# A backbone of two layers: scatters with a bound on the row, and the second layer's rows kept in the output tensor

## The chip, the cores and the metric

The kernel runs on one core of a Trainium2 chip. The metric is the device time of one execution in microseconds (us); lower is better. The core has a matrix engine (TensorE, PE in the rows), a vector engine (VectorE, DVE), an activation engine (ScalarE, ACT), GpSimd (POOL), SyncE (SP), which only issues transfers and waits, and 16 DMA engines that all queues share. Transfers issued by SyncE and ScalarE go over hardware queues (q1, q10), those of GpSimd over the software queue (q0).

## What is computed

Two layers over 1024 latent tokens of width 1024, in float32: a Fourier mixer, then a short gated convolution, each followed by a mixture of 16 experts of which every token uses two. Context tokens don't reach the output in this depth. Cut to what matters here:

```python
x = x + g1 * mixer(norm(x) * (1 + sc1) + sh1)          # layer 0: Fourier, layer 1: convolution
h = norm(x) * (1 + sc2) + sh2
comb = weights of the two chosen experts of each token   # (1024, 16), two entries per row
y = 0
for e in range(16):
    y = y + comb[:, e:e+1] * ((silu(h @ w_gate[e]) * (h @ w_up[e])) @ w_down[e])
x = x + g2 * y                                           # after layer 1 this is the output
```

## The kernel before, in words

**Stages.** Layer 0's Fourier mixer, its router, its experts; then layer 1's convolution, router and experts. After each mixer the residual rows x are stored in a tensor in device memory, x_dram[layer], and the normalized rows h in h_dram[layer]. Both are kept there because the experts read and add rows in an order that the router decides.

**The experts.** The 2048 pairs of a token and an expert are sorted by expert and cut into slots of 128 rows, an expert's pairs beginning a new slot. With 16 experts there are at most MAX_SLOTS = 31 slots; how many are used is read from a register, and the loops skip the others by twos. A slot's pairs fill its rows from row 0 on; the rows left over are padding. TOKI holds for each slot (a column) the token of each row (a partition), and for a padding row SEQ + partition, 1024 to 1151, by a minimum with the constant column C_SPARE.

Of each slot, GpSimd gathers its 128 rows of h into XG (line 577, four slots ahead), with a bound of SEQ - 1 on the row, so padding is skipped. TensorE transposes XG (line 1782), multiplies by gate and up weights (line 1792), transposes the hidden rows (line 1798) and multiplies by down weights (lines 1805, 1811). VectorE evicts the result, weighted, into one of two tiles YO (line 1370). GpSimd scatters YO with addition into x_dram[layer] (line 588); each scatter waits for the landing of the one before. Padding rows are added to 128 spare rows that x_dram has behind its 1024.

**SyncE's queue** holds the loads of expert weights in the order of the experts: gate and up into RAW (line 451), down into WDR (line 455), two buffers each, a load waiting until the buffer's expert is done. After layer 0's experts it reads x_dram[0] back into X (line 505). After layer 1's experts, line 528 copies the first 1024 rows of x_dram[1] to the output, as 64 pieces of 64 KB, and waits for that.

**Signals.** x_stored[layer] counts the stores of x (8 tiles) and the fill of the spare rows (`fill_spare_rows`, lines 416 to 419, issued by GpSimd near the start as ones from the constants K). y_scattered[layer] counts landings of scatters, moe_done is raised once all of a layer's have landed.

```python
if s:
    pool.wait_ge(y_scattered[layer], 16 * s)
    pool.sem_inc(y_added, 1)
pool.indirect_dma_start(out=x_dram[layer], out_offset=bass.IndirectOffsetOnAxis(ap=TOKI[:, s:s + 1], axis=0),
                        in_=YO[s % 2][:], in_offset=None, compute_op=ALU.add
                        ).then_inc(y_scattered[layer], 16)
```

Of the kernel before, what the change touches and what calls it, by code (L numbers as in the profile page):

```python
# [23 lines left out]
P = 128  # L24
SEQ, D = 1024, 1024
NT = SEQ // P
NC = D // P
# [98 lines left out]
def backbone(nc, x, c, w_ada, b_ada, norm_mix, norm_ffn, fourier_w_out, conv_w_in, conv_w, conv_w_out,  # L126
             router_w, router_bias, moe_w_gate, moe_w_up, moe_w_down, tables, constants, out):
    f32, f32r, i32, u32 = mybir.dt.float32, mybir.dt.float32r, mybir.dt.int32, mybir.dt.uint32
    ALU, ACT, X_AXIS = mybir.AluOpType, mybir.ActivationFunctionType, mybir.AxisListType.X
# [3 lines left out]
    def sem(name):  # L133
        return top.enter_context(nc.semaphore(name))
# [18 lines left out]
    x_rows, out_rows = x[0], out[0]  # L153
# [11 lines left out]
    ident, ones, lower = (K[:, a:a + P] for a in (C_IDENT, C_ONES, C_LOWER))  # L165
# [28 lines left out]
    r = Region(rows_at)  # L194
    FAB = r.put("FAB", [P, 2, D])
    FAA = r.put("FAA", [P, 2, D])
    r = Region(fourier_at)
# [12 lines left out]
    r = Region(fa_at)  # L210
# [3 lines left out]
    r = Region(fold_at)  # L214
# [3 lines left out]
    r = Region(fourier_at)  # L218
# [5 lines left out]
    r = Region(phase)  # L224
# [7 lines left out]
    r = Region(base)  # L232
    WDR = r.put("WDR", [P, 2, FF // P, D])
    XG = [r.put(f"XG{i}", [P, D]) for i in range(2)]
    YO = [r.put(f"YO{i}", [P, D]) for i in range(2)]
# [4 lines left out]
    r = Region(ada_at - width(SQ.shape))  # L240
# [6 lines left out]
    r = Region(ada_at)  # L247
# [49 lines left out]
    def bank(i, n=1):  # L297
# [1 line left out]


    h_dram = [nc.dram_tensor(f"h_dram{i}", [SEQ, D], f32, kind="Internal").ap() for i in range(2)]
    x_dram = [nc.dram_tensor(f"x_dram{i}", [SEQ + P, D], f32, kind="Internal").ap() for i in range(2)]


    consts_in, small_in, c_in, tables_in = sem("consts_in"), sem("small_in"), sem("c_in"), sem("tables_in")
    vectors_in, vectors_tr, warm = sem("vectors_in"), sem("vectors_tr"), sem("warm")
    bias_in, norm_row_in, out_done = (
        sem(n) for n in ("bias_in", "norm_row_in", "out_done"))
    wf_in = [sem(f"wf_in{i}") for i in range(2)]
    wm_in = [sem(f"wm_in{i}") for i in range(2)]  # L310
    wn_in = sem("wn_in")
# [101 lines left out]

        return 2 if layer == 0 and m % 2 else 4

    def fill_spare_rows(pool, layer):

        rows = x_dram[layer].rearrange("s (c n) -> s c n", n=P)
        pool.dma_start(rows[SEQ:SEQ + P, :, :], ones[:, None, :].to_broadcast([P, NC, P])).then_inc(x_stored[layer], 16)

    def slots_used(engine):

        return engine.value_load(SEID[0:1, MAX_SLOTS:MAX_SLOTS + 1], min_val=PAIRS // P, max_val=MAX_SLOTS)
# [2 lines left out]
    def _(sp):  # L426
# [30 lines left out]
        for layer in range(2):  # L457
            for m in range(0, NT, 1 if layer else 2):
                sp.wait_ge(h_ready, layer * NT + m + 1)
                sp.dma_start(rows_of(h_dram[layer], layer, m), h_tile(layer, m)[:]).then_inc(h_stored[m % 4], 16)  # L460
            sp.wait_ge(y_mm, NT * (layer + 1))
            load_gate_up(layer, 0, 0)
            load_gate_up(layer, 1, 1)
            sp.wait_ge(x_stored[layer], 16 * (NT + 1))
            load_down(layer, 0, 0)
            sp.wait_ge(routed, layer + 1)
            b = layer * MAX_SLOTS

            def after_split(e):
                sp.wait_ge(w_low, end_of(e) * PIECES + b * PIECES)  # L470

            def after_down(e):
                sp.wait_ge(yd_mm, end_of(e) + b)

            after_split(0)
            load_gate_up(layer, 2, 0)
            load_down(layer, 1, 1)
            after_split(1)
            load_gate_up(layer, 3, 1)
            after_down(0)  # L480
            load_down(layer, 2, 0)
            with sp.Fori(2, HALF) as j:
                for k in range(2):
                    after_split(2 * j + (k - 2))
                    load_gate_up(layer, 2 * j + k, k)
                    after_down(2 * j + (k - 3))
                    load_down(layer, 2 * j + (k - 1), 1 - k)
            after_down(EXPERTS - 3)
            load_down(layer, EXPERTS - 1, 1)
            if layer == 0:  # L490
                def load_win(j, part, par):

                    src = conv_w_in[0].rearrange("(c p) (s n) -> p c s n", p=P, s=3)[:, :, part, ds(j * P, P)]
                    sp.dma_start(WINR[par][:], src).then_inc(win_in[par], 16)

                def load_ada_pair(piece, half):

                    for k in range(2):
                        sp.wait_ge(wa_used, 4 * piece + (N_ADA + 2 * half + k - 1))
                        load_ada(sp, 1, piece, 2 * half + k, k)  # L500

                load_ada_pair(2, 0)
                sp.wait_ge(moe_done, 1)
                for m in range(NT):
                    sp.dma_start(X[:, m, :], x_dram[0][m * P:(m + 1) * P, :]).then_inc(x_back[m], 16)
                load_win(0, PARTS[0], 0)
                load_win(0, PARTS[1], 1)
                sp.wait_ge(cin_mm, 1)
                load_win(0, PARTS[2], 0)
                for n in range(3):  # L510
                    sp.wait_ge(cin_mm, n + 2)
                    load_win(1, PARTS[n], (n + 1) % 2)
                with sp.Fori(1, NC // 2) as i:
                    for k in range(2):
                        for n in range(3):
                            sp.wait_ge(cin_mm, 6 * i + (3 * k + n - 1))
                            sp.sem_inc(win_free, 1)
                            load_win(2 * i + k, PARTS[n], (k + n) % 2)
                            if n == 0:
                                load_ada_pair(i + (1 + k), 1 - k)  # L520
                load_ada_pair(5, 1)
                sp.wait_ge(cin_mm, 3 * NC)
                for q in range(4):
                    sp.dma_start(WOR[:, 2 * q:2 * q + 2, :],
                                 conv_w_out[0, 2 * q * P:2 * (q + 1) * P, :].rearrange("(j p) n -> p j n", p=P)
                                 ).then_inc(wout_in[q], 16)
        sp.wait_ge(moe_done, 2)
        sp.dma_start(out_rows.rearrange("(p r) d -> p (r d)", p=P),
                     x_dram[1][0:SEQ, :].rearrange("(p r) d -> p (r d)", p=P)).then_inc(out_done, 16)
        sp.wait_ge(out_done, 16)  # L530

    @block.gpsimd
    def _(pool):
# [5 lines left out]
        bias_row(0)  # L539

        pool.wait_ge(consts_in, 16)
        for layer in range(2):
            fill_spare_rows(pool, layer)

        pool.wait_ge(folds, 5)
        for g in range(GROUPS):
            pool.indirect_dma_start(out=WM[:, g, :], out_offset=None, in_=fourier_w_out[0],
# [34 lines left out]
        def scatter(layer, s):  # L582

            pool.wait_ge(yo_ready, s + (layer * MAX_SLOTS + 1))
            if s:
                pool.wait_ge(y_scattered[layer], 16 * s)
                pool.sem_inc(y_added, 1)
            pool.indirect_dma_start(out=x_dram[layer], out_offset=bass.IndirectOffsetOnAxis(ap=TOKI[:, s:s + 1], axis=0),  # L588
                                    in_=YO[s % 2][:], in_offset=None, compute_op=ALU.add
                                    ).then_inc(y_scattered[layer], 16)  # L590

        def slot(layer, s):
# [5 lines left out]
        for layer in range(2):  # L598
# [16 lines left out]
            gather(layer, 1, 1)  # L615
            pool.wait_ge(routed, layer + 1)
            used = slots_used(pool)
            pool.wait_ge(x_stored[layer], 16 * (NT + 1))
            if layer == 0:
                bias_row(1)  # L620
            for s in range(2):
# [1326 lines left out]
```

## Time and profile before

| what | value |
|---|---|
| median of 3 runs | 1252.8 us (1250.09 to 1255.69) |
| profiled execution | 1256.65 us, its span 1254.7 us |
| TensorE busy | 1119.3 us, 89% of the span |
| VectorE busy | 848.2 us, 68% |
| ScalarE busy | 490.6 us, 39% |
| GpSimd busy | 209.6 us, 17% |
| SyncE's and ScalarE's queues, GpSimd's queue | 38.2% and 2.9%, 18.0% of 16 DMA engines |
| chain that ended last | TensorE 69%, VectorE 9%, DMA 9%, issue 4%, ScalarE 4% |

The profile is one execution. The span runs from the first to the last record of the core. An engine's busy share doesn't tell what ends a stage; the chain of waits does, which is followed back from the last instruction to whatever released it. A transfer's time to landing runs from its issue to the moment when all 16 DMA engines have reported.

### The profile page before, as it was taken

What the parts mean: (1) busy time and instruction counts of PE and PEld (TensorE: products, weight loads), DVE (VectorE), ACT (ScalarE), POOL (GpSimd) and SP (SyncE); (2) the same over time, 40 slices, a digit from 0 to 9 for tenths busy, and PEclk for the clock granted to TensorE, in tenths of its full rate; (3) what the DMA queues carried; (4) which work ended last, traced back from release to release, by engine and by line L of the source; (5) the groups of instructions that cost most, each with busy time, mean ns of one, the idle gap of its engine ahead of it and who ended that gap; (6) DMA issues with size and microseconds to landing.
All of it is one profiled execution on the core that took longest, in us unless ns stands there. A gap on an engine that the chain in (4) does not pass through costs nothing.

```text
span 1254.7 us, 16332 instructions
## 1 busy us (share of the span) xinstructions
PE 1119.3 (89%) x4749; PEld 821.8 (65%) x4750; DVE 848.2 (68%) x976; ACT 490.6 (39%) x676; POOL 209.6 (17%) x140
## 2 busy tenths in 40 slices
PE   3999998899799899769999999979997799889991
PEld 1544456666567677458888888848885677667761
DVE  4886987789798799364444444463656788599782
ACT  5210233555556566341111111142222466476661
POOL 2201120322323333100000000000000132223331
PEclk9989999799989999879999999989998699999996
DMA  9859235489979987701333323231225569998946
GB/s 372 339 203 384 114 130 222 164 271 291 372 213 293 339 256 213 202 1 51 118 118 117 115 104 116 101 150 51 98 88 201 224 199 301 345 318 259 305 91 168
DMA packets 82170, 251.39 MB, mean 200 GB/s; under 512 B 8640, under 2 KB 33416, under 8 KB 73740
## 3 DMA queue, kind: packets, MB, share of 16 engines
q1 hardware_dynamic: 59604, 180.48, 38.2%
q0 software_dynamic: 18784, 56.69, 18.0%
q10 hardware_dynamic: 3736, 13.65, 2.9%
q8 instruction: 23, 0.38, 0.1%
q14 instruction: 23, 0.19, 0.0%
HBM read 220.39 MB, written 46.14 MB: 212 GB/s over the span
## 4 chain that ended last, share of the span: by engine, by line
PE 69%; DVE 9%; DMA 9%; issue 4%; ACT 4%; DVEq 1%; ACTq 1%; SPq 1%; POOL 0%; POOLq 0%
PE PS L1792 15%; PE PS L1700 7%; PE PS L1896 7%; PE PS L1900 7%; PE PS L1897 7%; DMA RAW<-in_moe_w_up_dram 6%; PE PS L1805 4%; PE PS L1811 3%; PE PS L1782 3%; PE PS L1568 2%; PE PS L1651 2%; PE PS L1668 2%; PE PS L1713 2%; DVE WL L1356 2%; ACT WH L842 1%
## 5 line engine op out<-in xcount | busy, mean ns | idle before, releaser
L1356 DVE TENSOR_TENSOR WL<-RAW,WH 128x1024 fp32r<-128x1024 f32 x204 | 240.0, 1219 | 37.7 <-ACT WH L842 31.1
L842 ACT ACTIVATE WH<-RAW 128x1024 fp32r x196 | 196.4, 1054 | 55.0 <-DMA RAW<-in_moe_w_up_dram 47.7
L1792 PE MATMUL PS<-WH,XTH 128*128 128x512 f32 x384 | 160.0, 417 | 20.7 <-DVE XTL L1349 11.8
L1896 PE MATMUL PS<-HTH,WINH 128*128 128x512 f32 x384 | 150.7, 393 | 5.4 <-DVE HTL L1476 5.4
L1792 PE MATMUL PS<-WL,XTH 128*128 128x512 f32 x384 | 155.4, 405 | 0.0
L1792 PE MATMUL PS<-WH,XTL 128*128 128x512 f32 x384 | 155.4, 405 | 0.0
L1897 PE MATMUL PS<-HTL,WINH 128*128 128x512 f32 x384 | 149.9, 390 | 0.0
L588 POOL DMA_INDIRECT x_dram<-YO,TOKI x46 | 99.1, 2154 | 300.1 <-DVE YO L1370 128.3
L1900 PE MATMUL PS<-HTH,WINL 128*128 128x512 f32 x384 | 118.7, 390 | 0.0
L1792 PEld LDWEIGHTS PS<-WH,XTH 128*128 128x128 f32 x384 | 75.7, 197 | 40.8 <-issue 25.9
L1041 DVE SCALAR_TENSOR_TENSOR ACC<-WA,SC,ACC 128x1024 f32 (+1 forms) x72 | 92.4, 1283 | 7.4 <-DMA WA<-in_w_ada_dram 3.2
L1805 PE MATMUL PS<-WDR,HETF 128*128 x184 | 88.4, 604 | 7.5 <-DVE YO L1370 7.5
L567 POOL DMA_DIRECT2D x_dram<-X x12 | 6.6, 553 | 502.2 <-DVE X L1112 433.9
L577 POOL DMA_INDIRECT XG<-h_dram,TOKI x54 | 68.5, 1269 | 125.9 <-PE PS L1782 64.8
L1792 PEld LDWEIGHTS PS<-WH,XTL 128*128 128x128 f32 x384 | 75.5, 197 | 16.9
L1896 PEld LDWEIGHTS PS<-HTH,WINH 128*128 128x128 f32 x384 | 72.3, 188 | 21.7 <-DVE HTL L1476 4.8
L1792 PEld LDWEIGHTS PS<-WL,XTH 128*128 128x128 f32 x384 | 75.6, 197 | 14.8
L1900 PEld LDWEIGHTS PS<-HTH,WINL 128*128 128x128 f32 x384 | 72.4, 188 | 15.1
L1897 PEld LDWEIGHTS PS<-HTL,WINH 128*128 128x128 f32 x384 | 72.4, 189 | 14.8
L1349 DVE TENSOR_TENSOR XTL<-PS,XTH 128x1024 fp32r<-128x1024 f32 x50 | 61.0, 1221 | 22.6 <-ACT XTH L833 22.5
L833 ACT ACTIVATE XTH<-PS 128x1024 fp32r<-128x1024 f32 x50 | 51.2, 1025 | 54.8 <-PE PS L1782 54.2
L929 ACT ACTIVATE WINH<-WINR 128x1024 fp32r<-128x1024 f32 x24 | 25.4, 1060 | 112.9 <-DMA WINR<-in_conv_w_in_dram 112.9
(230 smaller groups left out, 1737.0 us busy)
## 6 DMA issues: line engine op xcount, KB each, us to landing
RAW<-in_moe_w_gate_dram SPq DMA_DIRECT2D x32, 1024.0 KB
RAW<-in_moe_w_up_dram SPq DMA_DIRECT2D x32, 1024.0 KB
WDR<-in_moe_w_down_dram SPq DMA_DIRECT2D x32, 1024.0 KB
WA<-in_w_ada_dram SPq DMA_DIRECT2D x28, 1024.0 KB
WAE<-in_w_ada_dram SPq DMA_DIRECT2D x12, 1024.0 KB, 12.0
WINR<-in_conv_w_in_dram SPq DMA_DIRECT2D x24, 512.0 KB, 3.8
WA<-in_w_ada_dram ACTq DMA_DIRECT2D x8, 1024.0 KB
x_dram<-X POOLq DMA_DIRECT2D x12, 512.0 KB, 2.9
```

Source lines behind the costliest of these rows:

```text
L577: pool.indirect_dma_start(out=XG[par][:], out_offset=None, in_=h_dram[layer], in_offset=bass.IndirectOffsetOnAxis(ap=TOKI[:, s:s + 1], axi ...
L588: pool.indirect_dma_start(out=x_dram[layer], out_offset=bass.IndirectOffsetOnAxis(ap=TOKI[:, s:s + 1], axis=0), in_=YO[s % 2][:], in_offse ...
L842: nc.scalar.activation(piece_of(WH[par], i), raw_piece(e, i), ACT.Copy).then_inc(w_high, 1)
L1041: ins = V.scalar_tensor_tensor(out=dst, in0=WA_ALL[par][:, k, :], scalar=SC[:, at:at + 1], in1=dst, op0=ALU.mult, op1=ALU.add)
L1349: V.tensor_tensor(XTL[:].rearrange("p c n -> p (c n)"), bank(0, 2), XTH[:].rearrange("p c n -> p (c n)").bitcast(f32), ALU.subtract).then_ ...
L1356: V.tensor_tensor(piece_of(WL[par], i), raw_piece(e, i), piece_of(WH[par], i).bitcast(f32), ALU.subtract).then_inc(w_low, 1)
L1700: ins = T.matmul(bank(b + h), z[m % 2][:, ch, :], w[:, ch, h * BANK:(h + 1) * BANK], start=ch == 0 and i == 0, stop=ch == NC - 1 and i == 2)
L1792: ins = T.matmul(bank(2), x[:, ch, :], w[par][:, :, ch, :], start=ch == 0 and i == 0, stop=ch == NC - 1 and i == 2)
L1805: T.matmul(bank(4 + h), HETF[:], W[:, h * BANK:(h + 1) * BANK], start=True, stop=False)
L1896: T.matmul(bank(b), WINH[par][:, ch, :], HTH[:, ch, cols], start=ch == 0, stop=False)
L1897: T.matmul(bank(b), WINH[par][:, ch, :], HTL[:, ch, cols], start=False, stop=False)
L1900: ins = T.matmul(bank(b), WINL[par][:, ch, :], HTH[:, ch, cols], start=False, stop=ch == NC - 1)
```

## The change

Four edits that belong together. x_dram[0] has 1024 rows instead of 1152, and x_dram[1] is the output tensor itself. Each scatter has a bound of SEQ - 1 on the row and skips rows above it. The fills of the spare rows and their count in x_stored go. The copy from x_dram[1] to the output and the wait for it go; SyncE still waits for moe_done. TOKI and everything on TensorE, VectorE and ScalarE stay as they are.

```diff
-    x_dram = [nc.dram_tensor(f"x_dram{i}", [SEQ + P, D], f32, kind="Internal").ap() for i in range(2)]
+    x_dram = [nc.dram_tensor("x_dram", [SEQ, D], f32, kind="Internal").ap(), out_rows]
...
-    def fill_spare_rows(pool, layer):
-
-        rows = x_dram[layer].rearrange("s (c n) -> s c n", n=P)
-        pool.dma_start(rows[SEQ:SEQ + P, :, :], ones[:, None, :].to_broadcast([P, NC, P])).then_inc(x_stored[layer], 16)
...
-            sp.wait_ge(x_stored[layer], 16 * (NT + 1))
+            sp.wait_ge(x_stored[layer], 16 * NT)
...
         sp.wait_ge(moe_done, 2)
-        sp.dma_start(out_rows.rearrange("(p r) d -> p (r d)", p=P),
-                     x_dram[1][0:SEQ, :].rearrange("(p r) d -> p (r d)", p=P)).then_inc(out_done, 16)
-        sp.wait_ge(out_done, 16)
...
-        for layer in range(2):
-            fill_spare_rows(pool, layer)
-
...
-                                    in_=YO[s % 2][:], in_offset=None, compute_op=ALU.add
+                                    in_=YO[s % 2][:], in_offset=None, bounds_check=SEQ - 1, oob_is_err=False,
+                                    compute_op=ALU.add
...
-            pool.wait_ge(x_stored[layer], 16 * (NT + 1))
+            pool.wait_ge(x_stored[layer], 16 * NT)
```

On SyncE, the end of the program, behind the loop over the experts of layer 1. Before, the load of the last down weights is followed by the copy and the wait for it:

```order
190 L473 REGISTER_ALU
191 L455 DMA WDR<-in_moe_w_down_dram 128x2x1024 [waits yd_mm]
192 L528 DMA out_dram<-x_dram 64x16384 [waits moe_done]
193 L1924 UNCONDITIONAL_BRANCH [waits out_done]
```

After, the block ends on moe_done:

```order
190 L467 REGISTER_ALU
191 L449 DMA WDR<-in_moe_w_down_dram 128x2x1024 [waits yd_mm]
192 L1913 UNCONDITIONAL_BRANCH [waits moe_done]
```

One transfer and one wait have left the queue, and nothing stands in their place.

On GpSimd, the last scatters of layer 1 and the end of its program, before and then after:

```order
198 L588 DMA x_dram<-YO_109,TOKI 1152x1024 [waits yo_ready,y_scattered1]
199 L588 DMA x_dram<-YO_110,TOKI 1152x1024 [waits yo_ready,y_scattered1]
200 L588 DMA x_dram<-YO_109,TOKI 1152x1024 [waits yo_ready,y_scattered1]
201 L636 UNCONDITIONAL_BRANCH [waits y_scattered1]
```

```order
196 L576 DMA out_dram<-YO_109,TOKI 1024x1024 [waits yo_ready,y_scattered1]
197 L576 DMA out_dram<-YO_110,TOKI 1024x1024 [waits yo_ready,y_scattered1]
198 L576 DMA out_dram<-YO_109,TOKI 1024x1024 [waits yo_ready,y_scattered1]
199 L625 UNCONDITIONAL_BRANCH [waits y_scattered1]
```

The order and the waits are the same; the target is out, and 1024 rows are in reach instead of 1152.

## Rows read from the trace of the kernel before

**Rows 1.** The page: its head, TensorE's busy time, the chain that ended last.

```profile
span 1254.7 us, 16332 instructions
...
PE 1119.3 (89%) x4749; PEld 821.8 (65%) x4750; DVE 848.2 (68%) x976; ACT 490.6 (39%) x676; POOL 209.6 (17%) x140
...
PE 69%; DVE 9%; DMA 9%; issue 4%; ACT 4%; DVEq 1%; ACTq 1%; SPq 1%; POOL 0%; POOLq 0%
```

**Rows 2.** The chain's last stretch in order of time: start us, us, what.

```profile
1209.25 5.48 PE PS L1792 x24
...
1218.93 5.49 PE PS L1792 x24
...
1230.55 1.29 DVE YO L1370
...
1232.66 1.58 POOL x_dram L588
```

**Rows 3.** SyncE's instructions at the end: start us, us, engine, line, operation.

```profile
1239.07 0.63 SPq L528 DMA_DIRECT2D out_dram<-x_dram  x1
```

**Rows 4.** What SyncE waited for: us in total, times, longest us.

```profile
SPq L528 <- POOLq L644: 43.2, 1, 43.2
...
SPq L1924 <- DMA out_dram<-x_dram: 14.6, 1, 14.6
```

**Rows 5.** DMA traffic from 1232 to 1255: queues, then issues with us to landing.

```profile
q1 hardware_dynamic: 80, 4.19, 54.7%
q0 software_dynamic: 144, 0.52, 15.1%
...
x_dram<-YO,TOKI POOLq DMA_INDIRECT x1, 6.2
out_dram<-x_dram SPq DMA_DIRECT2D x1, 15.2
```

**Rows 6.** Line 567, the stores of x: duration ns min/median/max, then landing.

```profile
L567 POOL DMA_DIRECT2D x_dram<-X x12: 531/540/615, 127.6 to 947.4; - x12
...
DMA to landing us min/median/max: 2.9/2.9/5.1
```

**Rows 7.** Line 588, the scatters: both layers, landing, then layer 1 alone.

```profile
L588 POOL DMA_INDIRECT x_dram<-YO,TOKI x46: 1575/1866/4218, 253.5 to 1232.7; - x46
...
DMA to landing us min/median/max: 6.0/9.1/14.1
...
L588 POOL DMA_INDIRECT x_dram<-YO,TOKI x22: 1575/1828/4203, 1011.0 to 1232.7; - x22
```

**Rows 8.** DMA traffic from 1206 to 1212, with the packets' sizes.

```profile
DMA packets 288, 0.52 MB, mean 87 GB/s; under 512 B 160, under 2 KB 160, under 8 KB 288
```

**Rows 9.** The chain's transfers in the expert loops and between the layers.

```profile
257.19 10.52 DMA RAW<-in_moe_w_up_dram
...
320.70 14.48 DMA RAW<-in_moe_w_up_dram
...
413.92 11.99 DMA RAW<-in_moe_w_up_dram
...
508.07 6.58 DMA x_dram<-YO,TOKI
...
516.55 7.09 DMA X<-x_dram
...
1058.46 12.40 DMA RAW<-in_moe_w_up_dram
...
1082.93 13.05 DMA RAW<-in_moe_w_up_dram
...
1161.72 12.57 DMA RAW<-in_moe_w_up_dram
```

**Rows 10.** Busy times of two stretches; the last three columns: clock, DMA share, GB/s.

```profile
1058.00:1072.00 14.00, 14.00 (x63) 10.53 (x61) 7.69 (x9) 5.23 (x7) 3.60 (x3) 1.00 0.96 329
...
1161.00:1175.00 14.00, 14.00 (x63) 10.31 (x62) 10.48 (x12) 8.21 (x11) 3.49 (x2) 1.00 0.97 311
```

**Rows 11.** DMA traffic of the same stretches, 1058 to 1072, then 1161 to 1175.

```profile
q0 software_dynamic: 288, 0.85, 25.0%
...
x_dram<-YO,TOKI POOLq DMA_INDIRECT x2, 11.4
...
q0 software_dynamic: 420, 1.47, 37.9%
...
x_dram<-YO,TOKI POOLq DMA_INDIRECT x1, 11.5
```

**Rows 12.** Indirect transfers without a bound (564, 572) and with (577): ns min/median/max.

```profile
L564 POOL DMA_INDIRECT x_dram<-X,K x4: 973/1390/1885, 128.8 to 185.7; - x4
...
L572 POOL DMA_INDIRECT h_dram<-H,K x4: 950/954/1542, 164.9 to 195.4; - x4
...
L577 POOL DMA_INDIRECT XG<-h_dram,TOKI x54: 984/1040/2079, 219.1 to 1226.1; - x54
```

**Rows 13.** GpSimd's last two instructions, with the idle time before each.

```profile
1226.07 1.02 POOL L577 DMA_INDIRECT XG<-h_dram,TOKI  x1 [1.28 <-PE PS L1782]
1232.66 1.58 POOL L588 DMA_INDIRECT x_dram<-YO,TOKI  x1 [5.57 <-DVEq L1415]
```

**Rows 14.** GpSimd near the start: the fills of spare rows, the next work.

```profile
19.32 1.83 POOL L419 DMA_DIRECT2D x_dram<-K  x2 [12.36 <-DMA K<-in_constants_dram]
32.12 2.24 POOL L547 DMA_INDIRECT WM<-in_fourier_w_out_dram,K  x1 [10.98 <-DVE FAB L1027]
```

**Rows 15.** VectorE's first use of the WA blocks.

```profile
35.71 5.31 DVE L1041 SCALAR_TENSOR_TENSOR ACC<-WA,SC,ACC 128x1024 f32<-128x1024 f32 x4
```

More of the change, by code:

```diff
@@ L301, in backbone @@
     h_dram = [nc.dram_tensor(f"h_dram{i}", [SEQ, D], f32, kind="Internal").ap() for i in range(2)]
-    x_dram = [nc.dram_tensor(f"x_dram{i}", [SEQ + P, D], f32, kind="Internal").ap() for i in range(2)]
+    x_dram = [nc.dram_tensor("x_dram", [SEQ, D], f32, kind="Internal").ap(), out_rows]
     consts_in, small_in, c_in, tables_in = sem("consts_in"), sem("small_in"), sem("c_in"), sem("tables_in")
     vectors_in, vectors_tr, warm = sem("vectors_in"), sem("vectors_tr"), sem("warm")
-    bias_in, norm_row_in, out_done = (
-        sem(n) for n in ("bias_in", "norm_row_in", "out_done"))
+    bias_in, norm_row_in = sem("bias_in"), sem("norm_row_in")
     wf_in = [sem(f"wf_in{i}") for i in range(2)]
```

## The prediction

> **What bounds the kernel now.** I read the page's head first: one core, a span of 1254.7 us, TensorE busy for 89% of it, and TensorE with 69% of the chain of work that ended last; DMA holds 9% of that chain [rows 1]. The profiled execution took 1256.65 us, so 1.95 us lie around the span. That execution is 3.85 us above the median of 1252.8 us, so I work out a difference on its trace and take it off the median.
>
> The second view is the chain at its end. The last matrix products of the last slot lead to the eviction of YO (1230.55, 1.29 us) and to GpSimd's last scatter, issued at 1232.66 [rows 2]. The third view is SyncE's queue: the next thing in the program is one transfer, out from x_dram, issued at 1239.07 [rows 3], and the only thing after it is SyncE's 14.6 us wait for that transfer [rows 4]. The landing times say the same: the last scatter lands 6.2 us after its issue (1232.66 + 6.2 = 1238.9), the copy 15.2 us after its own (1239.1 + 15.2 = 1254.3), and the span ends 0.4 us later [rows 3, 5]. From 1238.9 no compute engine works; the end of the kernel is a serial transfer.
>
> **The copy of the output goes.** In after, layer 1 stores its rows in out and adds the experts' rows there, so the transfer of line 528 has no successor: SyncE waits for moe_done and the block ends. Of the old tail, 1239.1 to 1254.3 disappears, and the 0.4 us from the last landing to the end of the span stay. That is 15.2 us, all of it on the path, with no cover to look for and nothing late next except the last scatter, which was there before. Eight stores of 512 KB (x_dram from X, 540 ns each on GpSimd, 2.9 us to landing) change their destination and nothing else [rows 6]. Term: **-15.2 us**.
>
> A rule of the Trainium skill can be set beside this row. DMA: Bandwidth & Descriptors, "Anatomy of one DMA", fits a transfer from GpSimd's queue as 2.0 us plus its bytes at 436 GB/s; for the 4.19 MB that the copy moves this would be 11.6 us, where the trace has 15.2 [rows 5]. By the page the kernel would gain 3.6 us less; the row decides, since it is the very transfer that is removed.
>
> **The rows that pad a tile.** The loop issues 46 scatters of 128 rows (22 of them in layer 1), 5888 rows, of which 2 x 2048 are pairs of a token and an expert [rows 7]. The other 1792 rows, 30%, are padding: before, they are added to 128 spare rows; now their index is above the bound and they are skipped. What a skipped row costs is seen in the gathers, which have the same bound already. The stretch 1206 to 1212 holds one whole scatter and a gather for a slot that isn't used: 160 packets under 512 B and 128 others, 0.52 MB in all [rows 8]. So 128 skipped rows became 128 tiny packets and moved nothing.
>
> What a full scatter costs the DMA engines is seen in 1232 to 1255, where it is all that the software queue carries: 144 packets take 15.1% of 16 engines over 23 us, 3.5 us of each engine [rows 5]. The padding of a mean scatter is 30% of that, 1.06 us. It pays only where a transfer ends last. The chain names the places: six waits for gate and up weights (RAW), of 10.52, 14.48, 11.99, 12.40, 13.05 and 12.57 us, 75.0 us together [rows 9]. In two of these stretches the DMA share is 0.96 and 0.97 [rows 10], so the engines really are full there, and software-queue traffic takes 25.0% and 37.9% of them [rows 11]. Of scatters, the first stretch issues 2 and the second 1, say 1.5 for each wait. If relief went straight to the waits it would be 6 x 1.5 x 1.06 = 9.6 us. The other bound is 0: a load of weights is complete only when its slowest engine is, and the padding isn't spread evenly, since a slot's pairs fill its tile from row 0 and padding is always the last rows. Below nothing it can't go by this term, as packets only become smaller. I take a fifth of the upper end, because all engines must be relieved for a wait to end earlier. Term: **-2 us**, bounds -9.6 and 0.
>
> The Trainium skill has a rule against this gain: DMA: Bandwidth & Descriptors, "The descriptor swizzle", gives each DMA engine eight fixed partitions, engines 0 to 7 those below 64 and 8 to 15 those above. By it engine 0 keeps its eight rows in every tile with 36 or more pairs, and the term would be near 0 (1237.6 us in all). The page of the profile doesn't tell engines apart, so no row here shows it.
>
> Outside these waits less padding buys nothing. The only scatter that the chain holds whole inside the program is the last of layer 0 (508.07, 6.58 us, followed by 7.09 us for the way back into X) [rows 9]. Counted with the reference's own router on its inputs, the last expert's last tile has 121 pairs in layer 0 and 58 in layer 1: 7 and 70 padding rows. The first gives nothing. The second could shorten the very last landing by up to 70/128 of 3.5 us, 1.9 us, or not at all if one engine has only real rows; that is inside the bounds above.
>
> **The bound on the row.** Each scatter now has its indices compared with 1023. GpSimd spends 1575 to 4218 ns on a scatter [rows 7]. The price of the comparison lies between rows with and without it: indirect transfers without a bound take at least 950 and 973 ns, gathers with one at least 984 [rows 12], and 1.02 us where every row is skipped (the last gather, at 1226.07) [rows 13]. That is 0.01 to 0.05 us a piece; a loss of 0.05 x 46 = 2.3 us would need all to be exposed. Only the last one of each layer is, since otherwise GpSimd stood idle before its scatter, for 5.57 us before the last one [rows 13]. So 0.1 us at most, taken as 0.
>
> **The two fills of spare rows** at 19.3 us go (two instructions, 1.83 us of GpSimd, 2 x 512 KB). Nobody waits: GpSimd's next work, WM, starts at 32.12 after an idle time of 10.98 us for VectorE's FAB, and VectorE takes the first WA blocks at 35.71 with no idle time before it [rows 14, 15]. The saved transfers make the loads that were already queued land earlier, ahead of any reader. The final wait for x_stored has one landing less to count, and that landing was some 30 us in. Term: 0.
>
> **Sum.** -15.2 - 2 + 0 + 0 = -17.2 us. The profiled execution would have taken 1256.65 - 17.2 = 1239.5 us (span 1237.5); the median comes to 1252.8 - 17.2 = **1235.6 us**, 1.4% faster.
>
> **Rivals.** *Relief where it counts* (chance 0.22). The slowest DMA engine in the RAW waits is one that serves last rows, and gets rid of most of its padding. For: a share of 0.96 leaves little but those waits to shorten, and in 1161 to 1175 the software queue has 38% of the engines. Against: nothing shows which engine is last. With 5 to 10 us instead of 2 the time is 1227.6 to 1232.6; I put it at 1230. The skill's DMA: Bandwidth & Descriptors ("DMA engines 7/15 usually slower") would favour this, as it names the engine with the highest partitions as a slow one.
>
> *The bound is dear, or out is a slightly slower target* (0.08): 1 to 3 us of the copy's gain are lost at the exposed scatters and in slots where the next scatter waits on a landing: 1238 to 1240. For it speaks that no trace here has bound and addition together.
>
> *Scatters into out become the bound* (0.04, slower). Each scatter waits for the landing of the one before, so a slot can't be shorter than issue plus landing. TensorE's slot is 9.7 us (1209.25 to 1218.93) [rows 2]; the last scatter landed in 6.2, the median in 9.1 [rows 5, 7]. If the output tensor took additions so slowly that a landing passes 9.7 us even in quiet slots, each of the 22 slots of layer 1 pays the excess: at 10.4 the copy's gain is used up (22 x 0.7 = 15.2), beyond 10.7 the kernel is slower by over 0.5%, and at 11.5, the figure beside full loads [rows 11], it is 1252.8 - 15.2 + 40 = 1277.6. Against: both tensors are device memory, and the copy wrote out at full share.
>
> *The tail comes back in another form* (0.04, no change): the end of the kernel waits for something that the copy hid, such as a late completion of writes to out. The price can be up to the copy's own 15.2 us: about 1250.
>
> **How the numbers follow.** The forecast as summed has 0.62, from 1233.6 to 1237.6. Relief 0.22, dear bound 0.08, no change 0.04, slower 0.04. The median itself stands on runs from 1250.09 to 1255.69, some 3 us either way. The range 1228 to 1240 holds the first three but for their edges. A measurement of this kernel can tell about 0.5%, 6.3 us, from no change. Faster by more than that: 0.62 + 0.22 + 0.08 = 0.92; same 0.04; slower 0.04.
>
> **What would show it.** In the profile after: no transfer from x_dram to out, and the span ending within half a microsecond of the last scatter's landing; the last scatter at 6.2 us or a little less to landing, and 1575 ns still the least that a scatter takes on GpSimd. The software queue should carry about 1792 x 4 KB = 7.3 MB less, plus 1 MB of fills. The six RAW waits tell the second term: 73 us in sum for my forecast, 65 for the rival. If scatters of layer 1 take longer to land than those of layer 0 in quiet slots, out is the slower target. My number is wrong if the end of the chain isn't the last scatter, or if the RAW waits lose more than 5 us.

## The result, and the profile after

| kernel | median | lowest to highest | runs |
|---|---|---|---|
| before | 1253.09 us | 1249.5 to 1260.78 | 7 |
| after | 1242.95 us | 1240.95 to 1245.62 | 7 |

The ratio of after to before is 0.9918, with a 95% interval of 0.9892 to 0.9944: 10.3 us faster, between 7.0 and 13.5. The forecast was 17.2 us less, and its range ended at 1240. The sign was right, the size was not. The profiled execution of after took 1242.95 us, the median itself, with a span of 1241.0 us.

The head of the page, the DMA queues, and the chain that ended last, after; they answer to [rows 1]:

```profile
span 1241.0 us, 16376 instructions
...
PE 1114.6 (90%) x4749; PEld 820.0 (66%) x4750; DVE 848.0 (68%) x976; ACT 491.1 (40%) x676; POOL 207.5 (17%) x138
...
q1 hardware_dynamic: 59524, 176.29, 37.5%
q0 software_dynamic: 18496, 48.32, 15.2%
...
PE 72%; DVE 9%; DMA 8%; issue 4%; ACT 3%; DVEq 1%; ACTq 1%; SPq 1%; POOL 0%; POOLq 0%
```

The software queue q0 carries 48.32 MB. In the page of before it carried:

```profile
q0 software_dynamic: 18784, 56.69, 18.0%
```

These are 8.37 MB less, as forecast (1792 rows of 4 KB and 1 MB of fills). So padding rows and fills are gone. The copy is gone from q1, which carried 180.48 MB before. The tail is where the surprise lies. The last piece of the chain of after, which answers to [rows 2]:

```profile
1226.90 1.57 POOL out_dram L576
```

What SyncE waited for in after (us in total, times, longest), answering to [rows 4]:

```profile
SPq L1913 <- POOLq L633: 42.6, 1, 42.6
...
SPq L1913 <- PEq L1913: 7.1, 1, 7.1
```

There is no wait for a copy, but there is a new one of 7.1 us in the line on which the program's block ends. The instructions of that line in after (duration ns min/median/max, first and last start in us) name its cause:

```profile
L1913 ACTq DRAIN  x1: 8/8/8, 1226.5 to 1226.5; - x1
L1913 PEldq DRAIN  x1: 8/8/8, 1226.7 to 1226.7; - x1
L1913 DVEq DRAIN  x1: 17/17/17, 1230.3 to 1230.3; - x1
L1913 SPq COMPARE_BRANCH  x1: 38/38/38, 1233.7 to 1233.7; - x1
L1913 POOLq DRAIN  x1: 7017/7017/7017, 1233.7 to 1233.7; - x1
L1913 SPq DRAIN  x1: 7/7/7, 1233.9 to 1233.9; - x1
L1913 SPq EVENT_SEMAPHORE  x1: 17/17/17, 1240.9 to 1240.9; - x1
```

Every engine ends its program with an instruction called DRAIN and then meets the others. Those of the other engines take 7 to 17 ns; GpSimd's starts when the last scatter has landed (1233.7) and takes 7017 ns. The others wait for it until 1240.9, where the span ends. The row names PEq as the releaser, since the wait is put down to the last to arrive at the meeting; the rows of the line show that it was GpSimd that came late. The same line in before:

```profile
L1924 POOLq DRAIN  x1: 7017/7017/7017, 1239.1 to 1239.1; - x1
L1924 SPq COMPARE_BRANCH  x1: 38/38/38, 1254.3 to 1254.3; - x1
L1924 SPq DRAIN  x1: 7/7/7, 1254.5 to 1254.5; - x1
```

It was there all the time, from 1239.1 to 1246.1, beside the copy, which ran until 1254.3. Taking the copy away uncovered it.

### The profile page after: what moved, and what is told of

It reads as the page before. It is cut to its first block, busy times and chain, and to the rows that moved or that the text cites. A ratio compares the mean times of both kernels' runs of the same rounds, so it can differ in the third digit from the quotient of the medians.

```text
span 1241.0 us, 16376 instructions
## 1 busy us (share of the span) xinstructions
PE 1114.6 (90%) x4749; PEld 820.0 (66%) x4750; DVE 848.0 (68%) x976; ACT 491.1 (40%) x676; POOL 207.5 (17%) x138
## 3 DMA queue, kind: packets, MB, share of 16 engines
q0 software_dynamic: 18496, 48.32, 15.2%
## 4 chain that ended last, share of the span: by engine, by line
PE 72%; DVE 9%; DMA 8%; issue 4%; ACT 3%; DVEq 1%; ACTq 1%; SPq 1%; POOL 0%; POOLq 0%
PE PS L1781 16%; PE PS L1689 7%; PE PS L1885 7%; PE PS L1889 7%; PE PS L1886 7%; PE PS L1794 4%; PE PS L1800 3%; DMA RAW<-in_moe_w_up_dram 3%; PE PS L1771 3%; PE PS L1557 2%; PE PS L1640 2%; PE PS L1657 2%; PE PS L1702 2%; DVE WL L1345 2%; DVE ACC L1030 1%
## 5 line engine op out<-in xcount | busy, mean ns | idle before, releaser
L565 POOL DMA_INDIRECT XG<-h_dram,TOKI x54 | 71.2, 1319 | 129.2 <-PE PS L1771 67.6
L1781 PEld LDWEIGHTS PS<-WL,XTH 128*128 128x128 f32 x384 | 75.2, 196 | 14.7
L576 POOL DMA_INDIRECT x_dram<-YO,TOKI x24 | 51.9, 2165 | 151.5 <-DVE YO L1359 123.2
L555 POOL DMA_DIRECT2D out_dram<-X x8 | 4.3, 543 | 432.7 <-DVE X L1101 432.7
```

Source lines behind the costliest of these rows:

```text
L565: pool.indirect_dma_start(out=XG[par][:], out_offset=None, in_=h_dram[layer], in_offset=bass.IndirectOffsetOnAxis(ap=TOKI[:, s:s + 1], axi ...
L1781: ins = T.matmul(bank(2), x[:, ch, :], w[par][:, :, ch, :], start=ch == 0 and i == 0, stop=ch == NC - 1 and i == 2)
```

## Experiments

Ratios are against the kernel before, which was timed in turn with each group of kernels on the same chip. Its own median lay between 1252.8 and 1255.9 us from group to group, so times of two groups are compared by their ratios. "Us less" is a ratio's distance from 1, times the median of the kernel before.

**after_again** is the changed kernel once more, the reference for no_copy, keep_copy and drain_early, which were timed with it on one chip.

> The changed kernel once more, beside the three others on one chip. Both theories: about 1243 us, 10 us under the kernel before (1253.1). It is the reference for the others: GpSimd's last instruction of the program (DRAIN, 7017 ns in both traces) starts when the last scatter has landed and ends at the end of the span.

Measured: 1244.25 us beside 1254.67 us; ratio 0.9907, 0.9873 to 0.9941. As expected.

**no_copy** is the kernel before without its copy; it leaves the output unwritten.

```diff
         sp.wait_ge(moe_done, 2)
-        sp.dma_start(out_rows.rearrange("(p r) d -> p (r d)", p=P),
-                     x_dram[1][0:SEQ, :].rearrange("(p r) d -> p (r d)", p=P)).then_inc(out_done, 16)
-        sp.wait_ge(out_done, 16)
```

> The kernel before, spare rows, fills and unbounded scatters included, without the copy at its end; it leaves the output unwritten. Theory D: the tail goes from 15.2 us to the 7.1 us of the DRAIN, 8.1 us under before, 1245.0 us. My prediction's step (only 0.4 us lie behind the last landing): 15.2 us under before, 1237.9 us.

Measured: 1246.61 us, ratio 0.9924 (0.9896 to 0.9951), so 9.5 us less than before (6.1 to 13.0). The 8.1 us of theory D lie in that interval, the 15.2 us of my step don't. The line on which its block ends shows the DRAIN in the open, with the end of the span behind it:

```profile
L1921 POOLq DRAIN  x1: 7017/7017/7017, 1240.5 to 1240.5; - x1
...
L1921 SPq EVENT_SEMAPHORE  x1: 17/17/17, 1247.7 to 1247.7; - x1
```

**keep_copy** is the other part alone: the bound, no spare rows, no fills, but a tensor of its own for layer 1 and the copy.

```diff
-    x_dram = [nc.dram_tensor("x_dram", [SEQ, D], f32, kind="Internal").ap(), out_rows]
+    x_dram = [nc.dram_tensor(f"x_dram{i}", [SEQ, D], f32, kind="Internal").ap() for i in range(2)]
...
         sp.wait_ge(moe_done, 2)
+        sp.dma_start(out_rows.rearrange("(p r) d -> p (r d)", p=P),
+                     x_dram[1][0:SEQ, :].rearrange("(p r) d -> p (r d)", p=P)).then_inc(out_done, 16)
+        sp.wait_ge(out_done, 16)
```

> One part of the change alone: bound on the row, no spare rows, no fills; layer 1 still collects its rows in a tensor of its own, and the copy to the output stays. Theory D with a small relief of the DMA engines: 2 us under before, 1251 us. Rival (large relief, as the last scatter starts 5.8 us earlier in the trace of after than in that of before): 5 to 6 us under before, about 1247.5 us. If the bound cost anything that shows: at or over 1253 us.

Measured: 1251.56 us, ratio 0.9977 (0.9953 to 1.0001): 2.9 us less than before, between 5.9 less and none. The small relief is favoured, the large one is just inside the edge. The run measures bound and relief together, so by itself it only excludes a bound that costs more than the relief brings. No_copy and keep_copy together give 9.5 + 2.9 = 12.4 us; after gained 11.7 on this chip. The two parts add up.

**pool_waits** makes GpSimd wait for the copy in the kernel before, so that its DRAIN can't hide.

```diff
             pool.sem_inc(y_added, 1)
             pool.sem_inc(moe_done, 1)
+        pool.wait_ge(out_done, 16)
```

> The kernel before, with one wait more: GpSimd waits for the copy to the output before its program ends, so that its closing DRAIN can't run beside the copy. Theory D (fixed 7.0 us, hidden under the copy in before): 7.0 us over before, about 1261.5 us, with a DRAIN of 7017 ns behind the copy. Rival (the DRAIN's length is what is left of GpSimd's own transfers, long landed by then): a DRAIN well under 1 us and the time of before, 1254.7 us.

Measured: 1259.97 us beside 1255.28, ratio 1.0048 (1.0025 to 1.0071): 6.0 us more, between 3.1 and 8.9. The DRAIN of 7014 ns stands behind the copy:

```profile
L1925 SPq DRAIN  x1: 7/7/7, 1251.3 to 1251.3; - x1
L1925 POOLq DRAIN  x1: 7014/7014/7014, 1251.3 to 1251.3; - x1
```

The last scatter was issued at 1229.6 and landed 6.4 us later, so this DRAIN starts 15 us after the last landing of GpSimd's own transfers. It is as long there as right behind a landing. It isn't the remainder of a transfer under way.

**drain_early** is after, with GpSimd's last wait given to SyncE.

```diff
             with pool.Else():
-                pool.wait_ge(y_scattered[layer], (used + (used & 1)) * 16)
+                if layer == 0:
+                    pool.wait_ge(y_scattered[layer], (used + (used & 1)) * 16)
                 pool.sem_inc(y_added, MAX_SLOTS - 2 * PAIR_LOOPS)
             pool.sem_inc(y_added, 1)
-            pool.sem_inc(moe_done, 1)
+            if layer == 0:
+                pool.sem_inc(moe_done, 1)
...
-        sp.wait_ge(moe_done, 2)
+        used = slots_used(sp)
+        with sp.If(used > 2 * PAIR_LOOPS):
+            sp.wait_ge(y_scattered[1], 16 * MAX_SLOTS)
+        with sp.Else():
+            sp.wait_ge(y_scattered[1], (used + (used & 1)) * 16)
+            sp.sem_inc(moe_done, 1)
```

> As after, but in layer 1 GpSimd no longer waits for the landing of the last scatter; SyncE does. Theory D (the 7.0 us of GpSimd's closing DRAIN is a fixed time that the copy hid and that is now in the open): the DRAIN starts right behind the issue of the last scatter, some 5.2 us earlier (in the trace of after 1228.5 instead of 1233.7), and the kernel takes 5.2 us less than after, about 1237.8 us. Rival (the DRAIN first waits until GpSimd's transfers have landed and then takes its 7.0 us): the DRAIN becomes about 12 us long and the time stays at 1243 us.

Measured: 1240.33 us, ratio 0.9877 (0.9845 to 0.991). The median is 3.9 us below that of after_again, but with 5 and 4 executions whose ranges overlap (1238.2 to 1245.0 and 1242.4 to 1245.3) the times alone don't prove a gain. Neither theory came true as written: the DRAIN starts before the landing and takes 9721 ns.

```profile
L1921 POOLq DRAIN  x1: 9721/9721/9721, 1231.2 to 1231.2; - x1
...
L1921 SPq DRAIN  x1: 7/7/7, 1236.5 to 1236.5; - x1
```

SyncE, which waits for the landing, is at its own DRAIN at 1236.5; GpSimd's ends at 1240.9. What SyncE waits for at the end is now

```profile
SPq L1921 <- PEq L1921: 4.7, 1, 4.7
```

4.7 us instead of 7.1. So 2.4 us of what the DRAIN does had been done before the landing. Spread_early below, built the same way, shows 4.7 us again, with a DRAIN of 7973 ns. In the traces the time from the issue of the last scatter to the end of the span falls from 1241.0 - 1226.9 = 14.1 us to 1241.2 - 1230.2 = 11.0 us; 0.4 us of that are a landing 0.4 us sooner (6.2 against 6.6 us).

**Six small programs** ask what the DRAIN is made of. In them SyncE copies x to the output as one transfer, and GpSimd issues a number of 512 KB loads into one tile, each waiting for the one before. They compute nothing of the backbone, and each was run once.

```python
for i in range(LOADS):
    pool.dma_start(T0[:], x_rows[(i % 8) * P:(i % 8 + 1) * P, :]).then_inc(loaded, 16)
    pool.wait_ge(loaded, 16 * (i + 1))
pool.wait_ge(copied, 16)
```

> Not the backbone: one core, SyncE copies x to the output in one transfer, GpSimd clears a tile, issues no transfer and waits for the copy. It asks how long GpSimd's closing DRAIN is. If it is 7.0 us in any program: 7.0. If it is the price of having issued transfers: under 0.5 us, like the DRAIN at the start of the traces (183 ns).

> Not the backbone: SyncE copies x to the output, GpSimd clears a tile, issues one load of 512 KB, waits for its landing and for the copy, and ends. Without any transfer of GpSimd the closing DRAIN took 41 ns. Theory D (a fixed price of having issued transfers): 7.0 us behind the copy, the kernel 7 us longer than the 18.04 us without. Rival (the DRAIN grows with the number of transfers or descriptors, 118 transfers in the backbone): well under 1 us.

> As micro_pool1, but 40 loads one after another. Theory D: again 7.0 us, no matter how many. Rival: longer than for one load.

> As micro_pool40, with 80 loads. The DRAIN took 41, 135 and 3327 ns behind 0, 1 and 40 transfers, 82 ns for each one more. Theory N (it grows with the number of GpSimd's transfers): 3327 + 40 x 82 = 6.6 us. Rival (it stops growing earlier, or depends on the kind of transfer, and the 7.0 us of the backbone have another source): 3.3 us again or anything else.

> As micro_pool80, with 130 loads, the number of transfers that GpSimd issues in the changed backbone (132 in the kernel before). Theory N with a cap (the backbone shows 7017 ns with 132 as with 130): 7.0 us. Without a cap 3327 + 90 x 82 = 10.7 us; the backbone's 7.0 us would then be another thing.

(The backbone issues 130 transfers on GpSimd after the change and 132 before; the 118 in one expectation was a wrong count.) The closing DRAINs with 0, 1, 40, 80 and 130 loads:

```profile
L33 POOLq DRAIN  x1: 41/41/41, 16.0 to 16.0; - x1
```

```profile
L33 POOLq DRAIN  x1: 135/135/135, 17.1 to 17.1; - x1
```

```profile
L33 POOLq DRAIN  x1: 3327/3327/3327, 166.3 to 166.3; - x1
```

```profile
L33 POOLq DRAIN  x1: 6599/6599/6599, 324.4 to 324.4; - x1
```

```profile
L33 POOLq DRAIN  x1: 1454/1454/1454, 520.6 to 520.6; - x1
```

Both fixed-price theories fall: the DRAIN grows by (6599 - 3327) / 40 = 82 ns for each transfer that GpSimd has issued, although every one has landed by then. And it doesn't grow for ever: with 130 it is 1454 ns, the worth of 17. Something had been put away on the way, some 113 transfers. The trace of this program shows where. What GpSimd was idle for before its loads (us in total, times), and the load behind the odd one (start us, us, idle time before it):

```profile
  DMA T<-in_x_dram: 440.3, 128
  issue: 6.1, 1
```

```profile
454.73 0.54 POOL L29 DMA_DIRECT2D T<-in_x_dram  x1 [6.05 <-issue]
```

Once, and only once, GpSimd stands still for 6.05 us where it mostly waits 3.2 to 3.6 us for a landing, and for nothing that the profile names. The load behind this pause is the 114th, so 113 had been issued: the number that the DRAIN gave. The program with 80 loads has no such pause.

**micro_pool1_unwaited** issues one load and lets GpSimd end at once.

> As micro_pool1, but GpSimd waits for nothing after it has issued the load, so its DRAIN starts at once, beside the copy of some 15 us. In drain_early the DRAIN was 9.7 us and ended 4.6 us after the last landing would be expected, in spread_early 8.0. If the DRAIN is 7.0 us behind the end of the engine's own work (writing the descriptors, 1 to 2 us): about 8 to 9 us, hidden under the copy, and the kernel takes 18 us. If it is 7.0 us behind the landing: about 10 us or more, still hidden.

Its DRAIN lasts as long as its transfer is under way (landing 14.7 us after the issue at 2.0):

```profile
L32 POOLq DRAIN  x1: 14832/14832/14832, 2.0 to 2.0; - x1
```

So GpSimd's DRAIN waits for its engine's transfers even where the program doesn't. (SyncE's copy ran at the same time, but it isn't what the DRAIN waits for: in before the DRAIN ended at 1246.1, beside a copy under way until 1254.3.) The kernel took 18.97 us beside 19.26 with the waits.

**extra20 and extra40** add tiny loads on GpSimd's queue to after, ahead of layer 1's stores, where the engine is idle for some 340 us.

```diff
+    SPENT = keep.put("SPENT", [P, 8])
     SQ = keep.put("SQ", [P, D])
...
             if layer:
+                for i in range(20):
+                    pool.dma_start(SPENT[:], tables[:, 0:8]).then_inc(spent, 16)
+                    pool.wait_ge(spent, 16 * (i + 1))
                 for m in range(NT):
                     store_x(layer, m)
```

> As after, with 20 tiny loads more on GpSimd's queue (4 KB each, into a tile that nobody reads) in the middle of the kernel, where GpSimd has nothing to do for 300 us. The DRAIN of 7017 ns would be (7017 - 41) / 82 = 85 transfers that are still to be put away. Theory N (a list that is put away at the end, and now and then on the way, when it is full: 130 transfers left only 1454 ns, the worth of 17, so it was emptied behind some 113): 20 more make 7017 + 20 x 82 = 8.66 us and the time 1.6 us longer. Rival (7.0 us is a ceiling in this kernel, or these transfers don't count): 7017 ns again.

> As extra20, with 40 tiny loads. Theory N: 85 + 40 = 125 passes 113, the list is emptied on the way and 12 are left: a DRAIN of about 1.0 us, and the kernel takes 6 us less than after, 1238 us. Rival: 7017 ns or 10.3 us, and 1244 to 1247 us.

Measured: one run of extra20 at 1252.1 us; extra40 1253.18 us, ratio 1.0007 (0.999 to 1.0024), where after stood at 0.9907 and 0.9918. So extra40 is 11 to 12 us slower than after, not 6 us faster. The DRAINs:

```profile
L1917 POOLq DRAIN  x1: 6527/6527/6527, 1243.3 to 1243.3; - x1
```

```profile
L1917 POOLq DRAIN  x1: 6404/6404/6404, 1243.3 to 1243.3; - x1
```

6527 ns with 20 and 6404 with 40. More transfers made it shorter, by 490 and 613 ns, but not in the way of the simple count. The length does respond to transfers issued more than 600 us earlier. Theory N's count fails in both (8.66 and about 1.0 us were expected), and so does the rival's 7017 ns; when the list is emptied in the backbone stays open.

The slowdown of both has nothing to do with the end. Their products of 128x512 take longer throughout, which the groups of the convolution show; first after, then extra40:

```profile
L1886 PE MATMUL PS<-HTL,WINH 128*128 128x512 f32 x384 | 149.9, 390 | 0.0
L1889 PE MATMUL PS<-HTH,WINL 128*128 128x512 f32 x384 | 118.8, 390 | 0.0
```

```profile
L1890 PE MATMUL PS<-HTL,WINH 128*128 128x512 f32 x384 | 151.1, 394 | 0.0
L1893 PE MATMUL PS<-HTH,WINL 128*128 128x512 f32 x384 | 120.6, 395 | 0.0
```

390 ns became 394 and 395, and TensorE is busy for 1126.8 and 1126.3 us in extra20 and extra40 against 1114.6 in after, which is the size of the loss. It is neither the loads nor the clock: the last of the loads was issued at 570.1 and 622.9 us, but between 650 and 830 us, at a granted clock of 1.00 in all three, these products still take 389 ns in after and 393 to 397 in the other two. What differs there is that SPENT takes 32 bytes of each partition and moves all tiles laid out behind it. That this is the cause is argued from two kernels that share it, and wasn't tried by itself.

**spread** asks on which DMA engines the padding falls. It is after with another order of a slot's rows on the partitions, so that padding is dealt out by fours to partitions that, by the Trainium skill's DMA: Bandwidth & Descriptors ("The descriptor swizzle"), belong to different DMA engines.

```diff
-    t[:, C_ROW:C_ROW + P] = -i
+    rank = np.zeros(P, np.int64)
+    n = 0
+    for k in range(8):
+        for e in range(16):
+            at = 64 * (e // 8) + 4 * (e % 8) + 32 * (k // 4) + k % 4
+            rank[at] = n
+            n += 1
+    t[:, C_ROW:C_ROW + P] = -rank
```

> As after, but a slot's rows are laid on the partitions in another order (the constant row numbers are permuted), so that by the Trainium skill's swizzle (DMA: Bandwidth & Descriptors, The descriptor swizzle) the padding of a tile is shared by all 16 DMA engines instead of falling on the engines of the last rows. Theory S (in the waits for RAW the slowest DMA engine is one that serves first rows, so the padding that after skips hardly helps): every engine now gets rid of its share of scatter and gather, about 1.5 us a slot, over the waits for RAW 5 to 9 us; 1236 to 1239 us. Rival (it doesn't matter which engine the padding falls on, or the order of rows has nothing to do with engines): the same as after, 1244 us.

Measured: 1237.78 us beside 1255.28, ratio 0.986 (0.9831 to 0.9889). After stood at 0.9907, so the order of rows alone is worth some 6 us (between 0.3 and 11.5, with both intervals taken into account); drain_early and spread_early, which differ in the same way, are 7.4 us apart by their ratios. The last scatter shows the effect by itself: it has the same 58 rows of tokens in both kernels. DMA traffic at the end of after, then at the end of spread (us to landing last):

```profile
out_dram<-YO,TOKI POOLq DMA_INDIRECT x1, 6.6
```

```profile
DMA packets 145, 0.25 MB, mean 19 GB/s; under 512 B 86, under 2 KB 86, under 8 KB 144
...
out_dram<-YO,TOKI POOLq DMA_INDIRECT x1, 5.0
```

In before, with all 128 rows moved, it took 6.2 us [rows 5]. Skipping 70 of 128 rows brought nothing while they were the last rows; dealt out over the partitions, the same skip brought 1.6 us. The other traces agree: 6.0 to 6.6 us in the six with the 70 rows skipped at the end, 5.0 and 4.4 us in the two with them dealt out (spread and spread_early). The swizzle of the Trainium skill fits these rows: by it the first 58 partitions give six of the 16 engines their full eight rows, and the dealt order gives none more than four.

The change also shows in the loads of weights. What ScalarE, which takes the first of the weights, waited for them (us in total, times, longest) in before, after and spread:

```profile
ACT WH L842 <- DMA RAW<-in_moe_w_up_dram: 47.7, 12, 7.3
```

```profile
ACT WH L831 <- DMA RAW<-in_moe_w_up_dram: 40.5, 13, 7.3
```

```profile
ACT WH L838 <- DMA RAW<-in_moe_w_up_dram: 30.9, 12, 7.1
```

The other traces fall in the same order: 48.5 and 50.0 us where padding is written (pool_waits, no_copy), 43.8, 43.9 and 48.1 where it is skipped at the end (keep_copy, after_again, drain_early), 33.0 where it is dealt out (spread_early). A second way lies beside it. GpSimd's waits for the landing of the scatter before come to 123.3 us in before, 101.4 in after and 45.2 in spread. How much of the gain goes which way isn't separated.

**spread_unbound** has the new order in the kernel before, with unbounded scatters and the copy, so that only the gathers' padding is dealt out.

> The kernel before with nothing but the permuted rows of the kernel spread: scatters are unbounded and write all 128 rows, the copy stays; only the gathers, which skip padding already, have their padding spread over the DMA engines. Spread gained 6.5 us over after. If that comes from scatters and gathers by their cost (3.5 us of each engine for a scatter, about half of that for a gather): a third of it, 2 us under before, 1253 us. Rival (it is all the gathers, or another effect of the order of rows such as where they lie in memory): 6 us under before, 1248.5 us. Or nothing at all: only the scatters matter.

Measured: 1250.88 us beside 1255.86, ratio 0.9963 (0.9938 to 0.9988): 4.6 us less, between 1.5 and 7.8. So the order does something for the gathers alone; the interval holds both the 2 and the 6 us, so how the gain divides stays open. GpSimd's waits for its scatters stay long (139.0 us), but ScalarE's for the weights are shorter than the 47.7 of before:

```profile
ACT WH L849 <- DMA RAW<-in_moe_w_up_dram: 42.3, 14, 6.9
```

**spread_early** has the new order and the early end together.

> The permuted rows of the kernel spread and the early end of GpSimd of the kernel drain_early together; a candidate for the fastest version. If both effects add up: spread's time less 3 to 4 us (drain_early measured 3.9 us under after), 1232 to 1236 us; if the permutation does nothing, 1240 us.

Measured: 1232.97 us beside 1255.28, ratio 0.9818 (0.979 to 0.9847). It is the fastest version here: 22.8 us less than before and, by the ratios, some 11 us less than after. Spread alone has 17.6 of them; the early end adds 4.8 us to it by the medians, with six executions each (1235.2 to 1240.3 and 1230.7 to 1236.5), where drain_early had 3.9. The effects add up.

## Why the prediction was wrong

**What bounds the kernel now.** Half right: the copy was serial and ended last. But I wrote that from 1238.9 no compute engine works. GpSimd did, on an instruction that isn't counted as busy.

**The copy of the output goes, -15.2 us.** The step that failed is "the 0.4 us from the last landing to the end of the span stay". This wrote the distance from the copy's landing to the end of the span over to the landing of the last scatter. Behind that landing GpSimd's DRAIN takes 7.0 us. From the issue of the last scatter to the end of the span before took 1254.7 - 1232.7 = 22.0 us and after 14.1: 7.9 us gained, where the sum has 15.2. No_copy, which changes nothing but the tail, gained 9.5 us (6.1 to 13.0). The question to ask was what is late next. I named the last scatter and didn't read what each engine does on the line where the block ends. The rival "the tail comes back in another form" named the right kind of thing, was given 0.04, and took the copy's whole 15.2 us as its price instead of reading one.

The fit of the Trainium skill that I set beside the copy (DMA: Bandwidth & Descriptors, "Anatomy of one DMA") gave 3.6 us less. That it came nearer to the measured gain was luck: the copy did take its 15.2 us, and what was lost lay behind it. Another page of the Trainium skill would have led me away from the cause: VectorE: DVE Perf Modes ("The DRAIN you can't avoid") puts the DRAINs that belong to a program's start and end at a constant of about 12 ns on all five engines. Four engines agree, with 7 to 17 ns; GpSimd's 7017 ns don't, nor do the 41 to 6599 ns of the small programs.

**The rows that pad a tile, -2 us.** Near in size: keep_copy has -2.9 us (-5.9 to +0.1), an interval that just holds 0. The fifth that I took of the upper end was a guess, and that it came so near is luck. The reason given is borne out: padding is always the last rows, and what skips it helps only in part. Spread confirms it from the other side, with some 6 us more once the padding is shared. The rival "relief where it counts", with 0.22, needed the engines of the last rows to be the slowest; then skipping alone would have brought what only spread brought. That outside the RAW waits less padding buys nothing held for the one trace that I read: in no_copy, landings of unbounded scatters hold 9.0% of the chain, eleven of them in layer 1, and in spread_unbound 5.5%, eight in layer 0. No trace with a bound has more than two such landings in its chain. The sum of the six waits isn't a measure that holds still: the chain of after goes over other loads in their place.

```profile
259.96 11.56 DMA WA<-in_w_ada_dram
...
333.23 9.88 DMA RAW<-in_moe_w_gate_dram
...
411.02 11.70 DMA RAW<-in_moe_w_up_dram
...
1063.22 6.03 DMA WDR<-in_moe_w_down_dram
...
1078.71 12.22 DMA RAW<-in_moe_w_up_dram
...
1166.83 13.86 DMA RAW<-in_moe_w_up_dram
```

They come to 65.3 us where [rows 9] had 75.0, though only four of them, 47.7 us, are waits for RAW. By the prediction's own test that is the large relief, or more. But the same kernel in after_again has 55.6 us of RAW waits, and before with one wait more (pool_waits) has 69.0 with no padding skipped. I should have offered a timed comparison of keep_copy's kind as the test and not this sum. Likewise the last scatter of after starts 5.8 us earlier than in the trace of before, but that trace was of an execution 3.6 us above the median.

**The bound on the row, 0.** Right: the shortest scatter takes 1571 ns in after and 1575 in before [rows 7], the last one 1.57 against 1.58 us.

```profile
L576 POOL DMA_INDIRECT x_dram<-YO,TOKI x24: 1578/1876/4153, 254.4 to 506.1; - x24
L576 POOL DMA_INDIRECT out_dram<-YO,TOKI x22: 1571/1724/4041, 1008.5 to 1226.9; - x22
```

Those are GpSimd's own times. The landings are the test that the prediction set for the target: in after the median is 7.1 us in layer 0 and 9.2 us in layer 1, whose target is out. But keep_copy, with a tensor of its own for layer 1, has the same 7.1 and 9.2 us. So the output tensor takes additions as fast as the other one, and the rival on the slower side had nothing under it. (Its 22 x 0.7 is 15.4 and not 15.2, on which nothing hangs.)

**The fills, 0.** Not measured apart; keep_copy leaves them out too, so they are in its 2.9 us.

**The sum.** -8.1 for the tail (15.2 less the 7.1 us that came into the open) and -2.9 for the relief make -11.0 us. Measured were -10.3 (-7.0 to -13.5) in the first comparison and -11.7 (-7.4 to -15.9) in the second.

## What to carry to other kernels

When a transfer at the end of a kernel is removed, read what every engine does on the line on which the program ends, including instructions that aren't counted as busy; whatever ends next to last becomes the tail. Where GpSimd issues many transfers, let it reach its end early, and leave the last wait to an engine whose end is cheap; here that was worth some 4 us. Skipped padding rows helped little while they were always the last of the tile, and some 6 us more when they were dealt out over the partitions.

## What the runs showed of the hardware

- In the small programs GpSimd's closing DRAIN grows by 82 ns for each transfer that it has issued: 41, 135, 3327 and 6599 ns with 0, 1, 40 and 80. With 130 it is 1454 ns, and GpSimd stands still once for 6.05 us behind its 113th transfer. In the backbone it is 7017 ns with 130 as with 132 transfers, 6527 with 150 and 6404 with 170. What empties the list there is open.
- That DRAIN includes a wait for GpSimd's own transfers (14832 ns where one was under way). Started ahead of the last landing (drain_early, spread_early) it leaves SyncE 4.7 us to wait behind the landing and not 7.1.
- A scatter of 58 real rows and 70 skipped ones lands in 6.0 to 6.6 us with the skipped rows at the end, and in 5.0 and 4.4 us with them dealt out over the partitions; with all 128 written it took 6.2 to 6.4.
- In both kernels in which tiles lay 32 bytes further on (extra20, extra40), products of 128x512 in the convolution took 394 to 395 ns instead of 390, and TensorE was busy for 12 us more. The link to the address is argued, not shown.
